# Latent attention in a two-block transformer kernel: finer waits before the scores, and the next queries' second half turned one head later

## What is computed

```python
def gqa_block(qblk, k, v):
    s = jnp.einsum('bqkgd,bskd->bkgqs', qblk, k, preferred_element_type=jnp.float32) * ATTN_SCALE
    p = jax.nn.softmax(s, axis=-1).astype(v.dtype)
    return jnp.einsum('bkgqs,bskd->bqkgd', p, v)
```

## Time and profile before

| | |
|---|---|
| median of 3 runs | 3812.17 us (3805.87 to 3814.03) |
| the profiled execution's own time | 3812.06 us |
| its span | 3810.3 us |
| PE busy over the span | 3464.8 us (91%) |
| DVE, ACT, POOL busy | 2214.7, 1740.2, 1401.2 us |
| scores of the latent attention, first and last matmul L1393 | 1753.3 and 2091.9 us |
| output matmuls L1427, last | 2102.9 us |
| granted PE clock, mean | 0.942 |

### The profile page before, as it was taken

The page is one execution under the profiler, slowest core; times in us unless marked ns, Lnnn a source line. Parts: engine busy times, 40 slices in busy tenths (PEclk is TensorE's granted clock), DMA queues, the critical chain, the costliest instruction groups (busy, mean ns, idle before and its releaser), DMA issues. The chain is left out here.

```text
span 3810.3 us, 59174 instructions
## 1 busy us (share of the span) xinstructions
PE 3464.8 (91%) x18690; PEld 3042.7 (80%) x18690; DVE 2214.7 (58%) x4502; ACT 1740.2 (46%) x4132; POOL 1401.2 (37%) x1828
## 2 busy tenths in 40 slices
PE   5999988899999999797999929999999949999998
PEld 4899877899999987586888727888787748888786
DVE  5466767355677775435777175666435566666334
ACT  1277511667777771324555153333334463333333
POOL 2365323455566763313331334444001224444000
PEclk8999989899999998898999959999999769999999
DMA  3311255211122214300000022222354012222354
GB/s 145 127 40 39 101 221 220 87 42 42 59 62 64 63 61 160 129 1 28 1 0 0 22 107 76 83 83 83 127 197 150 29 49 83 83 83 83 127 198 143
DMA packets 97166, 332.99 MB, mean 87 GB/s; under 512 B 10673, under 2 KB 37601, under 8 KB 85090
## 3 DMA queue, kind: packets, MB, share of 16 engines
q1 hardware_dynamic: 96994, 330.90, 24.5%
HBM read 269.76 MB, written 61.10 MB: 87 GB/s over the span
## 5 line engine op out<-in xcount | busy, mean ns | idle before, releaser
L2062 PE MATMUL ps<-down_high,hidden_high 128*128 128x512 f32 x704 | 277.3, 394 | 13.5 <-DVE hidden_low L1963 13.2
L2045 PE MATMUL ps<-columns_combined,up_high_even 128*128 128x512 f32 x616 | 243.7, 396 | 46.4 <-POOL up_low_even L1830 32.7
L2063 PE MATMUL ps<-down_low,hidden_high 128*128 128x512 f32 x704 | 275.8, 392 | 0.0
L2064 PE MATMUL ps<-down_high,hidden_low 128*128 128x512 f32 x704 | 275.5, 391 | 0.0
L374 PE MATMUL ps<-w_hi,hT_hi 128*128 128x512 f32 x640 | 254.2, 397 | 22.5 <-DVE hT_lo L398 11.9
L1961 DVE TENSOR_TENSOR down_low<-down_raw,down_high 128x1024 fp32r<-128x1024 f32 x88 | 107.8, 1225 | 273.4 <-ACT down_high L1878 273.4
L375 PE MATMUL ps<-w_lo,hT_hi 128*128 128x512 f32 x640 | 252.8, 395 | 0.0
L376 PE MATMUL ps<-w_hi,hT_lo 128*128 128x512 f32 x640 | 252.1, 394 | 0.0
L2046 PE MATMUL ps<-columns_combined,up_high_even 128*128 128x512 f32 x616 | 242.9, 394 | 0.0
L2047 PE MATMUL ps<-columns_combined,up_low_even 128*128 128x512 f32 x616 | 242.5, 394 | 0.0
L2046 PE MATMUL ps<-columns_combined,up_high_odd 128*128 128x512 f32 x616 | 239.7, 389 | 0.0
(11 more groups left out here) (365 smaller groups left out, 9999.4 us busy)
## 6 DMA issues: line engine op xcount, KB each, us to landing
mod_weights<-in_w_mod SPq DMA_DIRECT2D x24, 2048.0 KB, 8.5
up_raw<-in_w_up SPq DMA_DIRECT2D x44, 1024.0 KB, 4.8
down_raw<-in_w_down SPq DMA_DIRECT2D x88, 512.0 KB, 3.6
hidden_columns<-hidden SPq DMA_DIRECT2D x44, 512.0 KB, 2.6
hidden_columns<-hidden_columns SPq DMA_DIRECT2D x88, 256.0 KB, 3.9
w_raw<-in_w_in_b SPq DMA_DIRECT2D x24, 768.0 KB, 4.5
group_rows<-unit_rows SPq DMA_DIRECT2D x64, 132.0 KB, 1.8
unit_rows<-group_rows SPq DMA_DIRECT2D x64, 132.0 KB, 2.1
```

Of the source, the lines that this page charges most:

```text
L2045: nc.tensor.matmul(out, a_hi, combined.moving(0, z, k), start=(start and k == 0), stop=False, **again)
L2062: nc.tensor.matmul(out, h_hi[:, s, t], down_hi[:, s, cols], start=begin, stop=False)
L2063: nc.tensor.matmul(out, h_hi[:, s, t], down_lo[:, s, cols], start=False, stop=False)
L2064: last = nc.tensor.matmul(out, h_lo[:, s, t], down_hi[:, s, cols], start=False, stop=end)
```

## The change

`scores` waits before each of its parts for the low part of that bank alone: one, two and three of the three subtractions. `turn_queries(1)`, `q_high(1)` and `q_low(1)` move from step `h` = 6 to step `h` = 7, on PE behind `out` and ahead of the scores of head 1 of the next tile, on ACT behind the exponential, on DVE behind the three low parts and ahead of `out`. This happens in tiles 0 to 6.

```diff
@@ scores
-                        if not first and part != 1:
+                        if not first:
 
-                            pe.wait_ge(core.probs_t_dve.sem, core.probs_t_dve.at(3 * (n - 2) + (2 if part == 0 else 3)))
+                            pe.wait_ge(core.probs_t_dve.sem, core.probs_t_dve.at(3 * (n - 2) + part + 1))
@@ tensor, tile
                         if some:
                             out(pe, p, j, h % 2)
-                        if next_queries:
+                        if more and h == QH2 - 1:
                             turn_queries(pe, t + 1, 1)
@@ scalar, tile
-                        if more and h == QH2 - 2:
-                            q_high(act, t + 1, 0)
-                            q_high(act, t + 1, 1)
+                        if more and h >= QH2 - 2:
+                            q_high(act, t + 1, h - (QH2 - 2))
@@ vector, tile
-                        next_queries = more and h == QH2 - 2
-                        if next_queries:
-                            q_low(dve, t + 1, 0)
-                            q_low(dve, t + 1, 1)
+                        if more and h >= QH2 - 2:
+                            q_low(dve, t + 1, h - (QH2 - 2))
                         if h % 2 and not (first and h < 2):
                             out(dve, p, *earlier(t, h))
```

## The result

| | before | changed |
|---|---|---|
| median (range) of 4 runs each | 3809.77 us (3805.87 to 3814.03) | 3783.36 us (3783.06 to 3790.86) |
| ratio, 95% interval | | 0.9936 (0.9924 to 0.9948) |
| span of the profiled execution | 3810.3 us | 3781.6 us |
| first score matmul of step 0, tile 0 | 1762.76 us | 1761.38 us |
| first score matmul of the last head | 2090.44 us | 2069.24 us |

The changed kernel is faster by 0.64%, some 24 us by the ratio; the medians are 26.4 us apart. The forecast was 3794.6 us, 17.5 less than before, and its range ended at 3789: right in direction, too small in size. The walk itself lost 19.8 us. Of the rest of the 28.7 us between the two profiled executions, 7.5 lie behind the walk, and the experiments show that these do not belong to the change.

A forecast was written before the change was run, and what follows sets the result against it. PE was taken as busiest, held up by waits for DVE's second low part. Gains of 11.9 us (loop steps 1 to 7), 2.6 (step 0), 0.9 (tile 7) and 2.1 (tile 0) made 17.5: 3794.6 us, range 3789 to 3805.

The forecast's parts named there:

- What bounds the kernel: Walk over the heads: PE is busiest, but some 22 us are not its work; scores wait for DVE's second low part.
- PE's floor is 4.73 us for odd and 4.94 for even steps: Loop tile: PE's own work per step, against scores then 0.45 us late in odd and 0.10 in even steps.
- It is covered: Heads 1 and 3: DVE's extra work makes the maximum 0.13 us late, but next scores come at 9.30 against PE's 9.67.
- the fourth rival: Odd steps: another wait, such as DVE's preparation, takes over; half of their 9.7 us gain is lost, 3799.5 us; chance 0.11.
- The new wait: Ahead of the second part's scores: costs 0, upper bound 0.11 us; as a rival 6.8 us, 3801.4 us, chance 0.12.
- Half 1 one head later: Steps 6 and 7: scores of step 6 start 0.41 us earlier; step 7 takes 5.14 us against 5.16, gaining 0.02.
- Step 7's handshake: Step 7: ACT's and DVE's work after the moved transposes ends at 7.15 us, before the maximum's 7.19, hidden by 0.04.
- part 1: Scores: a wait for each part gains 0.51 us in step 0, 0.45 in odd steps, 0.10 in steps 2 and 4.
- The sum: Whole walk: 11.9 and 2.6 us in loop tiles, 0.9 in tile 7, 2.1 in tile 0; together 17.5, giving 3794.6.
- The range: Total time: 3789 to 3805 us, taking in the two middle rivals and the spread, leaving out the last two.
- The slower rivals: Handshake of step 7 not hidden: 3809.6 us, chance 0.08; granted clock falls to 1.2 GHz at step 6: 3827.7, chance 0.03.

The follow-up runs named there:

- the kernel with the longest wait: Against the changed kernel, each score part waits for all three low parts: 3824.47 us, ratio 1.0045.
- with POOL out of the way: Against the changed kernel, POOL's sum for the next queries waits until DVE's two products of head 4 are done: 3787.25 us, ratio 0.9944.
- the second comparison: The changed kernel run once more with no edit: 3791.41 us, ratio 0.9953 to the kernel before.

## Why the prediction was right or wrong, point by point

- **What bounds the kernel**: right. The waits alone bring the gain, and with all three low parts asked for, DVE's chain gives the odd steps and step 0 to 0.02 us (3.84 + 1.68 = 5.52 and 4.11 + 1.68 = 5.79, measured 5.50 and 5.78).
- **"PE's floor is 4.73 us for odd and 4.94 for even steps"**: the step that failed. The floor was taken from steps that began with a stall, and held the 0.11 us that a group of score matmuls loses after one (0.34 against 0.23). It is 4.61 and 4.83: the waits-only kernel shows it without the move, and the kernel with the longest wait brings the stalls and the 0.34 us back. Of the five ordinary steps at the floor (0 to 4) four gained 0.10 to 0.12 more each than forecast; step 0 gained 0.03 more, as the half turned in step 7 costs it 0.08. In tile 0 (steps 1 to 7) and tile 7, where I counted even steps as 0 since the view draws no idle time there, it is the same: they lost 2.2 and 1.9 us, against 1.5 and 0.9 forecast.
- **"It is covered", of DVE's extra work**: right in steps 1 and 3. Head 4's products were named in the fourth rival but never worked out, and I took durations as fixed. The first product took 1.07 us before, 1.47 after, and 0.685 with POOL out of the way. This took back 0.35 us in step 5 and 0.09 in step 6 of each of six tiles. The fourth rival (another wait takes over in odd steps) named the place; its price was 4.9 us, of which 2.7 came true.
- **The new wait**: taken at 0, and it is 0, with seven such waits as with one.
- **Half 1 one head later**: the gain of step 6 was put at 0.41 us, measured 0.31 in the move alone: in the loop the scores start 0.09 later behind the stall than the transposes did. Step 7's handshake is hidden as worked out: `q_high` starts 5.37 us after the scores of step 6 (1878.27 − 1872.90; 5.42 forecast), `q_low` 6.00 (6.05), and the maximum 2.04 after the scores. The sum counted step 7 rightly, at 0.02. But "they fill the wait that part 1 would have removed" hides what the move is worth: a stall that is removed anyway is no cover, and against the waits-only kernel the move costs 0.7 us.
- **The sum**: 17.5 us forecast, of which 0.6 lie ahead of the walk; so 16.9 against the 19.8 measured in the walk. The two errors have opposite signs. With the clash out of the way the walk loses 22.5 us, so the terms that hang on the floor were 5.6 us short, and the clash hid 2.7 of that, which was luck. The whole change in total time was 24 us in one comparison and 18 in the next (ratios 0.9936 and 0.9953, with intervals that overlap).
- **The range**: too tight on its low side. It had the bounds of the added costs and none for the floor, where the 0.11 us stood in the earlier trace rows as the price of another thing: 0.11 × 62 = 6.8 us less would have been 3787.8. And the stages behind, with their clock, move the total by up to 8 us between executions of one program. That the median fell below 3789 owes more to this than to the floor: less the 20.9 us between the first score matmul and that of the last head, the profiled execution before would have taken 3791.2 us, and the second comparison gave 3791.41, both inside the range.
- **The slower rivals**: the granted clock was 1.00 over the stretch of the walk, and the handshake was hidden.

## What to carry to other kernels

Read an engine's floor from steps in which it did not wait: what an instruction costs just behind a stall is part of the stall, and goes with it. When a stall is removed, look at once for work that had been placed in it or would be placed in it, since it is on the path from then on. Where two engines run pieces of one job, a faster loop changes which pieces meet, and durations are not constants.

## What the runs showed of the hardware

- A group of matmuls that starts right behind a stall has 0.34 us between its first two starts, where the same group whose wait was met has 0.23. The 0.11 us are the load of the first weights: it begins a matmul ahead where the wait was met (1860.97 for 1861.09) and only with the matmul's row where it wasn't (1866.05). The scores behind the four transposes of step 7 show nearly the same without any stall (0.32 us between the first two starts, the first load at 1877.96 for 1877.98); why the load isn't ahead there wasn't tried.
- 372 waits that are met cost nothing measurable on PE, also between single matmuls, and the loads of weights stay ahead across them.
- One DVE product of 128 × 512 with both inputs in SBUF takes 0.685 us alone and 1.47 us when 0.92 of it lie beside a POOL sum of 1.30 us. The Trainium skill, "SBUF — State Buffer", section "Who interferes with whom", says that a DVE instruction with two SBUF inputs contends with a GpSimd instruction that reads SBUF, as its second input comes through the shared read interface. The runs agree: DVE's low parts and maxima, which read PSUM and at most one input from SBUF, keep their 1.62 and 1.49 us beside POOL (in the changed kernel the low parts from 1876.74 beside POOL's L1498 from 1876.94; in the kernel with the move alone the maximum from 1904.75 beside POOL's L1483 from 1904.34).
- The same program took 1712.4 and 1720.4 us for the part behind the walk in two executions. Some 7.4 of the 8 us arise within one stretch of 41 us of the pool mixing, at whose end the granted clock was 1.00 in one execution and 0.76 in the other.
